# A hybrid decoder block: four projections stream 512 weight columns per matmul, tile by tile

## The chip, the cores and the metric

The kernel runs on one core of a Trainium2 chip. The metric is the device time of one execution in microseconds (us), less being better; the figure of a kernel is the median of its runs. A core has five engines with queues of their own: TensorE (PE), VectorE (DVE), ScalarE (ACT), GpSimd (POOL) and SyncE (SP), which here issues nearly all the loads. They meet only at semaphores.

## What is computed

One layer for 256 tokens of width 1024. `[u | q | k | v | g_pool | g_attn] = RMSNorm(x) @ W_in`; q, k and v feed a stick-breaking attention of 8 heads, u a pooling mixer; the two results are gated, summed into `merged`, and multiplied by `W_out`. Then a top-4-of-32 mixture of experts follows, whose weights (12 MB per expert) are nearly all the bytes that the kernel reads.

```python
h = rmsnorm(x, norm1_g)
u, q, k, v, g_pool, g_attn = split(h @ w_in)
merged = sigmoid(g_pool) * pool_out + sigmoid(g_attn) * attn_out
x = x + merged @ w_out
x = x + moe_ffn(rmsnorm(x, norm2_g), ...)
```

## The kernel before

**Blocks of weights.** The dense part works on twelve blocks of weights in the order q, k, v, u, gp0, gp1, pool_up, ga0, ga1, attn_up, out0, out1 (numbers 0 to 11). A block is 1024 x 512, 2 MB, and lies in SBUF as two halves of 256 columns, each half as eight rows k (one for each 128 of the contraction) of 256 columns. SP loads half h of block b with one DMA of 1 MB into buffer `raw[b % 5]`. ACT copies it to `w_hi[b % 2]` in the type fp32r (`split`, L496), and DVE subtracts that from `raw` in place, which gives `w_lo` (`split`, L626 by its helper). Each half that DVE has done counts in `s_lo` (name `rests_done`). The activations `act_in` have a first part and a rest as well, so a product takes three matmuls (`mm3`: first part by first part, first part by rest, rest by first part).

**The projections.** `project` handles q, k, v, out0 and out1, where the activations are the weights of the array (128 x 128) and the weight block streams past. T = 2 tiles of 128 tokens and KD = 8 rows k give, for each half of the columns, 16 products or 48 matmuls of 256 columns; a block takes 96. The first half goes row by row (k outside, tile inside) and needs only half 0 of the block; the second goes tile by tile and waits for half 1. After the first half PE counts `s_first`, after each tile of the second `done` (`s_proj` or `s_wo`). For out0 the first half takes rows k as `merged` appears (`merged_there`, semaphore `s_mrg`, name `merged_ready`). In v the transposes of the normed k (`transposed(kn)`, L1042) stand between the halves.

**The units.** Between v and out0 PE works through 20 units (attention, u, gates, pool_up, attn_up) in an order written out by hand. In the last four, attn_up, DVE forms `merged` from each unit and splits it in two (L626 onto `act_in`, which counts `s_mrg`); in DVE's program these come ahead of the second half of block 10, which is out0 (`split(10, TWO)`), and that ahead of both halves of block 11 (`split(11)`).

**Buffers and loads.** `used(b, h)` names the semaphore value at which half h of block b is free; SP waits for it before it loads block b + 5, and, since the expert ring `gate_ring` lies over the same memory, before each of 16 gate loads of 1 MB of the first two experts: the second expert's first four wait for out0's halves, its last four for out1's. Then come four loads into `down_ring` (1 MB each), and from there the expert loop: SP reloads a slot each time PE has used it (`s_gu`, `s_du`).

**After out1.** DVE adds x to the four output quarters (`x1`), PE transposes it, and a short chain of small steps on all engines finds the experts (router, ranks, places), after which PE enters the loop over pairs of experts.

Of the kernel before, what the change touches and what calls it, by code (L numbers as in the profile page):

```python
# [5 lines left out]
P = 128  # L6
# [18 lines left out]
def hybrid_block_kernel(nc, x, norm1_g, w_in, q_norm_g, k_norm_g, w_pool_grp, pool_scale, w_pool_up,  # L25
# [4 lines left out]
    T = S // P  # L30
    KD = D // P
# [22 lines left out]
    with ExitStack() as ctx:  # L54
# [49 lines left out]
        NRAW, NHI, BW = 5, 2, KD * BLK  # L104
# [7 lines left out]
        w_lo = [buffer(f"w_lo{j}", j, F32R) for j in range(NRAW)]  # L112
        w_hi = [buffer(f"w_hi{j}", HI_AT + j, F32R) for j in range(NHI)]
# [22 lines left out]
        kn = carve(area_m, 2176, T, BLK)  # L136
# [49 lines left out]
        bank = [ctx.enter_context(nc.psum_tensor(f"bank{i}", [P, 512], F32)) for i in range(8)]  # L186
# [6 lines left out]
        BLOCKS = ["q", "k", "v", "u", "gp0", "gp1", "pool_up", "ga0", "ga1", "attn_up", "out0", "out1"]  # L193
# [11 lines left out]
        s_proj, s_first = sem("projected"), sem("first_half_projected")  # L205
# [6 lines left out]
        s_wo, s_x1, s_hn = sem("out_proj_done"), sem("x1_ready"), sem("hn_ready")  # L212
# [33 lines left out]

        def used(b, h):

            if BLOCKS[b] in ("q", "k", "v"):
                return (s_first, b + 1) if h == 0 else (s_proj, 2 * b + 2)  # L250
            if BLOCKS[b] in ("out0", "out1"):
                return (s_first, b - 6) if h == 0 else (s_wo, 2 * b - 18)
            unit = UNITS.index((BLOCKS[b], 0))
            if BLOCKS[b] in ("pool_up", "attn_up"):
                return s_unit, unit + 2 * h + 2
            return s_unit, unit + h + 1
# [21 lines left out]
        PROJ = (6, 2, 4)  # L278
        TR = (0, 6)
# [691 lines left out]
        def _(pe):  # L971
# [8 lines left out]
            for k in range(KD):  # L980
                for t in range(T):
                    last = nc.tensor.transpose(bank[k // 2][:, (k % 2) * S + t * P:(k % 2) * S + (t + 1) * P],
                                               xn[:, t, k * P:(k + 1) * P], ident[:])
            last.then_inc(s_xT, 1)

            def mm3(o, stat, mov, start):

                mm(o, stat[0], mov[0], start)
                mm(o, stat[0], mov[1], False)
                return mm(o, stat[1], mov[0], False)  # L990
# [6 lines left out]
            def acts(k, cols_at=0, n=S):  # L997
                return act_in[:, 0, k, cols_at:cols_at + n], act_in[:, 1, k, cols_at:cols_at + n]

            def wait_split(b, h):  # L1000

                pe.wait_ge(s_lo, pieces(b)[h][2])

            HB = BLK // 2

            def project(b, banks, ready, done, between=None):

                for t, k in [(t, k) for k in range(KD) for t in range(T)]:
                    if t == 0:
                        ready(k)  # L1010
                        if b == 0 and k % 4 == 0:
                            pe.wait_ge(s_lo, k // 4 + 1)
                        if b and k == 0:
                            wait_split(b, 0)
                    last = mm3(banks[t][:, 0:HB], acts(k, t * P, P), weights(b, 0, k * HB, HB), k == 0)
                last.then_inc(s_first, 1)
                if between:
                    between()
                for t in range(T):
                    for k in range(KD):  # L1020
                        if t == 0 and b == 0 and k % 4 == 0:
                            pe.wait_ge(s_lo, k // 4 + 3)
                        if t == 0 and b and k == 0:
                            wait_split(b, 1)
                        last = mm3(banks[t][:, HB:BLK], acts(k, t * P, P), weights(b, 1, k * HB, HB), False)
                    last.then_inc(done, 1)

            def no_wait(k):
                pass

            def hT_there(k):
                pe.wait_ge(s_hT, k + 1)
# [5 lines left out]
            def transposed(src, b, count):  # L1038
                pe.wait_ge(s_qkn, count)
                for a in range(PAIRS):  # L1040
                    for t in range(T):
                        last = nc.tensor.transpose(  # L1042
                            bank[b + a // 2][:, (a % 2) * S + t * P:(a % 2) * S + (t + 1) * P],
                            src[:, t, a * P:(a + 1) * P], ident[:])
                last.then_inc(s_tr, 1)

            project(0, bank[PROJ[0]:PROJ[0] + T], hT_there, s_proj)
            project(1, bank[PROJ[1]:PROJ[1] + T], no_wait, s_proj)
            transposed(qn, TR[0], T)
            project(2, bank[PROJ[2]:PROJ[2] + T], no_wait, s_proj, lambda: transposed(kn, TR[1], 2 * T))  # L1050

            pe.wait_ge(s_const, 7)
            pe.wait_ge(s_qk, 6)
# [1 line left out]
            for n, (name, j) in enumerate(UNITS):  # L1055
                t = STEP.get(n, -1)
                if 0 <= t - 2 < PAIRS:

                    pe.wait_ge(s_prob, 2 * (t - 2) + 2)
                    for key in range(T):  # L1060
                        for half in range(2):
                            h = 2 * (t - 2) + half
                            o = bank[head_bank(h)][half * HD:(half + 1) * HD, :]
                            last = mm(o[:, key * P:S], vn[:, key, h * HD:(h + 1) * HD],
                                      attn_prob[:, half, key * S:(key + 1) * S - key * P], key == 0)
# [21 lines left out]
                for half in range(2):  # L1087
# [7 lines left out]
                    b = BLOCKS.index(name)  # L1095
# [14 lines left out]
                        last = mm3(dst, weights(b, j, k * HB + half * P, P), acts(k), half == 0 and k == 0)  # L1110
                last.then_inc(s_unit, 1)

            for n in range(2):
                project(BLOCKS.index(f"out{n}"), [acc[n], acc[2 + n]], no_wait if n else merged_there, s_wo)

            for t in range(T):
                pe.wait_ge(s_x1, t + 1)
# [166 lines left out]
```

## Time and profile before

| | |
|---|---|
| median of 3 runs | 1133.45 us (1132.58 to 1134.44) |
| the profiled execution: span | 1132.6 us |
| its own time | 1132.58 us, the lowest of the three |
| PE busy | 1026.0 us, 91% |
| DVE busy | 278.0 us, 25% |
| ACT busy | 187.8 us, 17% |
| DMA | 431.01 MB, mean 381 GB/s |

The profile is of one execution. Its page has the busy time of the engines, the span cut into 40 slices with the granted TensorE clock and the DMA rate, the chain of work that ended last, the costliest groups of instructions and the DMA issues. The trace behind it has each instruction with start, duration and what ended the idle time before it, and it can be asked for stretches of time. PE matmuls overlap: the distance between two starts is shorter than the duration of one.

### The profile page before, as it was taken

The page shows a single profiled execution, that of the slowest core. Times are in us where ns is not written, and L with a number is a line of the kernel's source. Part 1 is how long each engine was busy: PE and PEld are TensorE (multiplying, and loading weights), DVE is VectorE, ACT ScalarE, POOL GpSimd, SP SyncE. Part 2 cuts the span into 40 slices and gives each one's busy share as a digit, 9 for nine tenths or more (in the row PEclk, how much of TensorE's full clock was granted, in tenths as well). Part 3 has the DMA queues.
Part 4 walks back from the last instruction along what each step waited for, and adds up shares of the span by engine and source line. Part 5 has one row for each costly group of instructions (what it writes and reads, how often), then busy time and mean ns, then how long its engine had stood idle before and what let it go on. Part 6 is the DMA issues. An engine that isn't in the chain of part 4 may idle for free.

```text
span 1132.6 us, 14659 instructions
## 1 busy us (share of the span) xinstructions
PE 1026.0 (91%) x5749; PEld 479.0 (42%) x5749; DVE 278.0 (25%) x516; ACT 187.8 (17%) x252; POOL 22.2 (2%) x36
## 2 busy tenths in 40 slices
PE   6999997999999888999989898888888988888897
PEld 6989995333333232333333333232323232233332
DVE  5655886211111111111111111111111010111112
ACT  5477433011101010101010101000010100010101
POOL 3200002000000000000000000000000000000000
PEclk9999998999999999999999999999999999999999
DMA  9933578899999999999999999999999999999996
GB/s 315 322 121 126 186 291 340 327 418 419 417 417 417 418 418 413 417 419 418 418 419 418 417 417 418 417 418 418 417 417 418 417 419 418 418 419 419 418 417 247
DMA packets 97330, 431.01 MB, mean 381 GB/s; under 512 B 7884, under 2 KB 28896, under 8 KB 64512
## 3 DMA queue, kind: packets, MB, share of 16 engines
q1 hardware_dynamic: 97304, 430.76, 94.7%
q8 instruction: 13, 0.21, 0.1%
q14 instruction: 5, 0.04, 0.0%
q10 hardware_dynamic: 8, 0.00, 0.0%
HBM read 429.68 MB, written 1.05 MB: 380 GB/s over the span
## 4 chain that ended last, share of the span: by engine, by line
PE 39%; DMA 27%; SPq 24%; DVE 6%; issue 3%; ACT 0%; POOL 0%; ACTq 0%; DVEq 0%; POOLq 0%
PE bank L973 38%; DMA gate_ring<-in_w_gate_up_dram 22%; SPq L329 11%; SPq L386 9%; DMA down_ring<-in_w_down_dram 4%; SPq L370 3%; DVE area_x L954 1%; PE bank L1238 1%; DVE area_m L626 1%; DVE area_x L938 1%; DVE area_x L626 1%; DVE area_x L939 1%; SPq L378 0%; DMA area_x<-in_x_dram 0%; DVE down_ring L626 0%
## 5 line engine op out<-in xcount | busy, mean ns | idle before, releaser
L973 PE MATMUL bank<-gate_ring,area_m 128*64 128x512 f32 x2048 | 466.3, 597 | 49.1 <-DMA gate_ring<-in_w_gate_up_dram 49.1
L973 PEld LDWEIGHTS bank<-gate_ring,area_m 128*64 128x64 f32 x2048 | 140.0, 136 | 357.1 <-issue 206.9
L973 PE MATMUL bank<-down_ring,area_x 128*64 128x512 f32 x1024 | 230.5, 600 | 24.3 <-DVE area_x L954 13.7
L938 DVE TENSOR_SCALAR area_x<-bank 128x512 f32<-128x512 f32 x32 | 22.1, 692 | 743.2 <-PE bank L973 743.2
L973 PEld LDWEIGHTS bank<-down_ring,area_x 128*64 128x64 f32 x1024 | 72.3, 137 | 163.8 <-issue 142.4
L973 PE MATMUL bank<-area_m 128*128 128x128 bf16 (+4 forms) x1024 | 121.9, 277 | 1.3 <-ACT area_m L609 1.3
L601 ACT ACTIVATE area_x<-area_x 128x512 f32<-128x512 f32 x32 | 20.2, 630 | 489.9 <-DVE area_x L938 489.9
L973 PEld LDWEIGHTS bank<-area_m 128*128 128x128 bf16 (+3 forms) x1024 | 77.5, 114 | 55.9 <-issue 52.1
L609 ACT ACTIVATE area_m<-bank 64x512 f32<-64x512 f32 x64 | 37.8, 591 | 311.4 <-PE bank L973 311.0
L973 PE MATMUL bank<-w_hi,act_in 128*128 128x256 f32 x320 | 59.9, 288 | 1.5 <-DVE act_in L662 1.5
L973 PE MATMUL bank<-act_in,w_hi 128*128 128x256 f32 x320 | 58.4, 284 | 0.0
L626 DVE TENSOR_TENSOR w_lo<-raw,w_hi 128x2048 fp32r<-128x2048 f32 (+1 forms) x26 | 54.7, 2127 | 6.4 <-ACT w_hi L496 6.1
L973 PEld LDWEIGHTS bank<-w_hi,act_in 128*128 128x128 f32 x320 | 51.3, 196 | 1.9 <-DVE act_in L662 1.9
L973 PEld LDWEIGHTS bank<-act_in,w_hi 128*128 128x128 f32 x320 | 49.8, 192 | 0.2 <-DVE area_m L757 0.2
L496 ACT ACTIVATE w_hi<-raw 128x2048 fp32r<-128x2048 f32 (+1 forms) x26 | 45.2, 1778 | 7.6 <-DMA raw<-in_w_in_dram 4.1
L973 PE MATMUL bank<-w_lo,act_in 128*128 128x256 f32 x160 | 45.9, 287 | 0.0
L973 PE MATMUL bank<-act_in,w_lo 128*128 128x256 f32 x160 | 45.3, 283 | 0.0
L973 PEld LDWEIGHTS bank<-w_lo,act_in 128*128 128x128 f32 x160 | 31.4, 196 | 0.0
L973 PEld LDWEIGHTS bank<-act_in,w_lo 128*128 128x128 f32 x160 | 30.7, 192 | 0.0
L954 DVE COPY area_x<-bank 128x512 f32<-128x512 f32 x32 | 22.1, 692 | 27.9 <-PE bank L1238 27.9
L1238 PE MATMUL bank<-ident,area_x 128*128 128x128 f32 x128 | 19.6, 276 | 9.9 <-DVE area_x L626 9.9
L626 DVE TENSOR_TENSOR area_m<-bank,cols 128x512 f32<-128x512 f32 x34 | 23.2, 684 | 2.4 <-PE bank L973 2.4
(171 smaller groups left out, 477.0 us busy)
## 6 DMA issues: line engine op xcount, KB each, us to landing
gate_ring<-in_w_gate_up_dram SPq DMA_DIRECT2D x256, 1024.0 KB, 20.1
down_ring<-in_w_down_dram SPq DMA_DIRECT2D x128, 1024.0 KB, 23.4
raw<-in_w_in_dram SPq DMA_DIRECT2D x16, 1024.0 KB, 10.2
raw<-in_w_out_dram SPq DMA_DIRECT2D x4, 1024.0 KB, 5.1
raw<-in_w_pool_up_dram SPq DMA_DIRECT2D x2, 1024.0 KB, 11.6
raw<-in_w_attn_up_dram SPq DMA_DIRECT2D x2, 1024.0 KB, 4.9
area_x<-in_x_dram SPq DMA_DIRECT2D x2, 512.0 KB, 3.8
out_dram<-gate_ring SPq DMA_DIRECT2D x4, 256.0 KB, 2.1
```

Source lines behind the costliest of these rows:

```text
L329: sp.dma_start(gate_ring[:, s, :], w_gate_up[0, bass.ds(e, 1), c * P:(c + 1) * P, :].rearrange("a p n -> (a p) n")) \
L370: sp.dma_start(down_ring[:, c], down_src(2 * i + half - 1, c)).then_inc(s_dl[c], 16)
L386: sp.dma_start(down_ring[:, c], down_src(e, c)).then_inc(s_dl[c], 16)
L496: nc.scalar.activation(w_hi[b % NHI][:, lo:lo + n], raw[b % NRAW][:, lo:lo + n], ACT.Copy) \
L601: nc.scalar.activation(sig, glu, ACT.Sigmoid, scale=ALPHA).then_inc(s_sig, 1)
L609: last = nc.scalar.activation(y_pair[half * SLOTS:(half + 1) * SLOTS, c * FH:(c + 1) * FH], y_b[c * SLOTS:(c + 1) * SLOTS, :], ACT.Copy)
L626: return nc.vector.tensor_tensor(o, a, b, op)
L938: nc.vector.tensor_scalar(glu, glu_b[:], LIMIT, None, ALU.min).then_inc(s_glu, 1)
L939: nc.vector.tensor_scalar(lin, lin_b[:], LIMIT, -LIMIT, ALU.min, ALU.max).then_inc(s_sr, 1)
L954: nc.vector.tensor_copy(actT, t_b[:].rearrange("p (a n) -> p a n", n=P)).then_inc(s_actT, 1)
L973: return nc.tensor.matmul(o, lhsT, rhs, start=start, stop=True, skip_group_check=True)
L1238: last = nc.tensor.transpose(t_b[:, c * P:(c + 1) * P], lin[:, c * P:(c + 1) * P], ident[:])
```

## The change

`project` is written anew. q keeps the old form under the name `project_halves`. k, v and out1 use the new `project`: it waits once for half 1 of the block (both halves are then there, since `s_lo` counts in order), and then does tile 0 whole and tile 1 whole, each as 24 matmuls of 512 columns; the moving operand takes 256 columns of row k from each half (`weights_row`). out0 uses `project_by_row`: the same matmuls, with k outside and the tile inside, and the waits for `merged` as before. A block takes 48 matmuls in place of 96. In v the transposes of kn stand after tile 0. `s_first` is counted only by q; `used` gives both halves of k, v, out0 and out1 free at the block's end.

```diff
         def used(b, h):
+            if b == 0 and h == 0:
+                return s_first, 1
             if BLOCKS[b] in ("q", "k", "v"):
-                return (s_first, b + 1) if h == 0 else (s_proj, 2 * b + 2)
+                return s_proj, 2 * b + 2
             if BLOCKS[b] in ("out0", "out1"):
-                return (s_first, b - 6) if h == 0 else (s_wo, 2 * b - 18)
+                return s_wo, 2 * b - 18
...
+            def weights_row(b, k):
+
+                return [w[:].rearrange("p (h x) -> p h x", h=2)[:, :, k * HB:(k + 1) * HB]
+                        for w in (w_hi[b % NHI], w_lo[b % NRAW])]
+
+            def project(b, banks, done, between=None):
+
+                wait_split(b, 1)
+                for t in range(T):
+                    for k in range(KD):
+                        last = mm3(banks[t][:].rearrange("p (h n) -> p h n", h=2), acts(k, t * P, P),
+                                   weights_row(b, k), k == 0)
+                    last.then_inc(done, 1)
+                    if between and t == 0:
+                        between()
+
+            def project_by_row(b, banks, ready, done):
+
+                wait_split(b, 1)
+                for k in range(KD):
+                    ready(k)
+                    for t in range(T):
+                        last = mm3(banks[t][:].rearrange("p (h n) -> p h n", h=2), acts(k, t * P, P),
+                                   weights_row(b, k), k == 0)
+                        if k == KD - 1:
+                            last.then_inc(done, 1)
...
-            project(0, bank[PROJ[0]:PROJ[0] + T], hT_there, s_proj)
-            project(1, bank[PROJ[1]:PROJ[1] + T], no_wait, s_proj)
+            project_halves(0, bank[PROJ[0]:PROJ[0] + T], hT_there, s_proj)
+            project(1, bank[PROJ[1]:PROJ[1] + T], s_proj)
             transposed(qn, TR[0], T)
-            project(2, bank[PROJ[2]:PROJ[2] + T], no_wait, s_proj, lambda: transposed(kn, TR[1], 2 * T))
+            project(2, bank[PROJ[2]:PROJ[2] + T], s_proj, lambda: transposed(kn, TR[1], 2 * T))
...
-            for n in range(2):
-                project(BLOCKS.index(f"out{n}"), [acc[n], acc[2 + n]], no_wait if n else merged_there, s_wo)
+            project_by_row(BLOCKS.index("out0"), [acc[0], acc[2]], merged_there, s_wo)
+            project(BLOCKS.index("out1"), [acc[1], acc[3]], s_wo)
```

On PE, at the start of out0, these stand in a row before; `bank0` and `bank2` are the two tiles' results, and `rests_done` is here half 0 of the block.

```order
L973 MATMUL bank7<-mix_in_61,w_hi1_60 128x256 x2
L973 MATMUL bank7<-mix_in_61,w_lo4_58 128x256
L973 MATMUL bank0<-w_hi0_59,act_in_62 128x256 [waits rests_done,merged_ready]
L973 MATMUL bank0<-w_lo0_54,act_in_62 128x256
L973 MATMUL bank0<-w_hi0_59,act_in_62 128x256
L973 MATMUL bank2<-w_hi0_59,act_in_62 128x256
L973 MATMUL bank2<-w_lo0_54,act_in_62 128x256
```

The same place on PE of the changed kernel.

```order
L975 MATMUL bank7<-mix_in_61,w_lo4_58 128x256
L975 MATMUL bank0<-w_hi0_59,act_in_62 128x512 [waits merged_ready,rests_done]
L975 MATMUL bank0<-w_lo0_54,act_in_62 128x512
L975 MATMUL bank0<-w_hi0_59,act_in_62 128x512
L975 MATMUL bank2<-w_hi0_59,act_in_62 128x512
L975 MATMUL bank2<-w_lo0_54,act_in_62 128x512
```

The order of the products is the same, each has 512 columns, and `rests_done` is now the count of half 1, whose instruction on DVE is the second half of block 10.

On DVE the instructions around it stand as before, in both kernels; these are the changed kernel's rows from the last part of `merged` on.

```order
L628 TENSOR_TENSOR area_m<-bank7,area_m 128x512 [waits attn_gate_ready,unit_done]
L628 TENSOR_TENSOR area_m<-area_m 128x512 [waits unit_evacuated]
L628 TENSOR_TENSOR act_in_62<-area_m,act_in_62 128x512 [waits merged_sum,merged_hi]
L628 TENSOR_TENSOR w_lo0_54<-raw0_49,w_hi0_59 128x2048 [waits first_parts_done]
L628 TENSOR_TENSOR w_lo1_55<-raw1_50,w_hi1_60 128x2048 [waits first_parts_done] x2
```

Nothing moved on DVE: PE's first matmul of out0 now waits for the `w_lo0` row here, which stands behind the last `act_in` row, and before it waited for a half done earlier.

## Rows read from the trace of the kernel before

**Rows 1.** Page, chain that ended last: shares of the span by engine and line

```profile
PE 39%; DMA 27%; SPq 24%; DVE 6%; issue 3%; ACT 0%; POOL 0%; ACTq 0%; DVEq 0%; POOLq 0%
```

**Rows 2.** Windows: stretch, its us, busy us of each engine, granted clock, DMA share, GB/s

```profile
158.50:194.00 35.50, 29.33 (x204) 23.56 (x203) 26.70 (x53) 10.28 (x15) 7.75 (x9) 0.87 0.99 401
194.00:203.00 9.00, 8.23 (x82) 6.10 (x82) 3.34 (x18) 1.87 (x2) 0.00 (x0) 0.93 0.03 14
206.00:1110.00 904.00, 821.81 (x4198) 299.40 (x4194) 138.25 (x280) 81.54 (x124) 0.00 (x0) 1.00 1.02 418
```

**Rows 3.** Timeline of SP's DMA issues, 145 to 203 us: start, us, line, tiles, count

```profile
147.76 18.09 SPq L325 DMA_DIRECT2D gate_ring<-in_w_gate_up_dram  x8
...
177.41 11.16 SPq L334 DMA_DIRECT2D down_ring<-in_w_down_dram  x4
202.73 0.36 SPq L329 DMA_DIRECT2D gate_ring<-in_w_gate_up_dram  x1
```

**Rows 4.** Timeline, PE and its weight loads (PEld), inside k

```profile
29.26 0.40 PE L973 MATMUL bank<-w_hi,act_in 128*128 128x256 f32 x2
29.38 0.19 PEld L973 LDWEIGHTS bank<-w_lo,act_in 128*128 128x128 f32 x1
29.50 0.28 PE L973 MATMUL bank<-w_lo,act_in 128*128 128x256 f32 x1
```

**Rows 5.** Timeline of PE at the head of the loop: 512 columns

```profile
200.65 13.91 PE L973 MATMUL bank<-gate_ring,area_m 128*64 128x512 f32 x64
214.49 3.70 PE L973 MATMUL bank<-area_m 128*128 128x512 f32 x8
```

**Rows 6.** Timeline of PE from the end of k to the attention

```profile
39.10 1.03 PE L1042 MATMUL bank<-ident,area_m 128*128 128x128 f32 x8
39.89 0.36 PE L973 MATMUL bank<-w_hi,act_in 128*128 128x256 f32 x1
...
45.72 1.04 PE L1042 MATMUL bank<-ident,area_m 128*128 128x128 f32 x8
...
53.27 0.89 PE L973 MATMUL bank<-area_m,down_ring 128*128 128x256 f32 x4 [0.78 <-ACT area_m L520]
```

**Rows 7.** Timeline of DVE, 19 to 52 us

```profile
19.86 4.70 DVE L626 TENSOR_TENSOR w_lo<-raw,w_hi 128x2048 fp32r<-128x2048 f32 x2 [0.27 <-ACT w_hi L496]
...
33.67 4.48 DVE L626 TENSOR_TENSOR w_lo<-raw,w_hi 128x2048 fp32r<-128x2048 f32 x2
...
40.00 0.69 DVE L674 TENSOR_REDUCE tiny<-down_ring 128x8 f32<-128x512 f32 x1 [1.25 <-ACT down_ring L516]
...
43.97 1.29 DVE L626 TENSOR_TENSOR area_m<-bank,tiny 128x512 f32<-128x512 f32 x2 [3.07 <-POOL tiny L416]
...
48.69 3.09 DVE L697 TENSOR_SCALAR down_ring<-bank,cols 64x512 f32<-64x512 f32 x4
```

**Rows 8.** Timeline of PE where out0 begins

```profile
153.33 0.28 PE L973 MATMUL bank<-w_hi,act_in 128*128 128x256 f32 x1
```

**Rows 9.** Timeline of DVE, 155 to 163 us

```profile
155.65 0.69 DVE L626 TENSOR_TENSOR act_in<-area_m,act_in 128x512 fp32r<-128x512 f32 x1 [0.70 <-ACT act_in L566]
156.26 6.69 DVE L626 TENSOR_TENSOR w_lo<-raw,w_hi 128x2048 fp32r<-128x2048 f32 x3
```

**Rows 10.** Timeline of PE, start of q

```profile
14.52 0.58 PE L973 MATMUL bank<-w_hi,act_in 128*128 128x256 f32 x1 [1.50 <-DVE act_in L662]
...
17.04 0.63 PE L973 MATMUL bank<-w_hi,act_in 128*128 128x256 f32 x2
...
17.68 0.47 PE L973 MATMUL bank<-w_hi,act_in 128*128 128x256 f32 x2
```

**Rows 11.** Timeline of PE between out1 and the loop

```profile
176.37 2.04 PE L1119 MATMUL bank<-ident,down_ring 128*128 128x128 f32 x16
...
189.50 0.21 PE L973 MATMUL bank<-area_m,below_bf 128*128 128x32 bf16 x1 [4.11 <-DVE area_m L845]
```

**Rows 12.** Windows, columns as in group 2

```profile
189.50:195.30 5.80, 5.80 (x27) 3.49 (x28) 3.55 (x19) 0.00 (x0) 0.00 (x0) 0.50 0.83 331
195.30:200.00 4.70, 4.13 (x54) 3.62 (x51) 3.34 (x18) 0.74 (x2) 0.00 (x0) 1.00 0.00 2
```

More of the change, by code:

```diff
@@ L1004, in _, with project_halves @@
             HB = BLK // 2
-            def project(b, banks, ready, done, between=None):
+            def project_halves(b, banks, ready, done):
                 for t, k in [(t, k) for k in range(KD) for t in range(T)]:
@@ L1010, in project @@
                         ready(k)
-                        if b == 0 and k % 4 == 0:
+                        if k % 4 == 0:
                             pe.wait_ge(s_lo, k // 4 + 1)
-                        if b and k == 0:
-                            wait_split(b, 0)
                     last = mm3(banks[t][:, 0:HB], acts(k, t * P, P), weights(b, 0, k * HB, HB), k == 0)
                 last.then_inc(s_first, 1)
-                if between:
-                    between()
                 for t in range(T):
                     for k in range(KD):
-                        if t == 0 and b == 0 and k % 4 == 0:
+                        if t == 0 and k % 4 == 0:
                             pe.wait_ge(s_lo, k // 4 + 3)
-                        if t == 0 and b and k == 0:
-                            wait_split(b, 1)
                         last = mm3(banks[t][:, HB:BLK], acts(k, t * P, P), weights(b, 1, k * HB, HB), False)
                     last.then_inc(done, 1)
-            def no_wait(k):
-                pass
+            def weights_row(b, k):
[19 more added lines that the diff above has]
+                            last.then_inc(done, 1)
             def hT_there(k):
```

## The prediction

> **What bounds the kernel now.** I read three views in this order. The chain that ended last gives PE 39% and the DMAs with their issues most of the rest [rows 1], which says only that the limit changes on the way. The windows say where: from 206 to 1110 us the DMA engines are full, at 418 GB/s, and PE, at 2.4 GHz throughout, has time to spare [rows 2]. So the loop over experts is a stream of bytes of fixed length, and nothing that PE does in it shortens it. But just before it, from 194 to 203 us, the DMA moves 14 GB/s [rows 2]: SP has issued its four loads of `down_ring` by 188.6 us and issues nothing until 202.73, when PE has used up the first gate slot [rows 3]. The rings are full and wait for PE. The end is therefore the start of the loop on PE (200 us) plus a fixed stream, and each us won or lost on PE's path up to 200 us counts whole. In the dense part PE runs from 53.27 us to 176.37 with no idle time before any instruction; its only waits between the start of q and out1's end are 1.5 us at 14.52 and 0.78 at 53.27 [rows 6, 10, 11]. The DVE and ACT steps of the units follow PE's and move with it. So the sum is made on PE.
>
> **The base.** The profiled execution took 1132.6 us, the lowest of the three; the median is 0.9 above it. The sum below is a difference to the profiled execution and is then put on the median.
>
> **Half as many matmuls, twice as long.** Each of four blocks (k, v, out0, out1) goes from 96 matmuls of 256 columns to 48 of 512. Before, starts are 0.12 us apart: two from 29.26 to 29.50 [rows 4], so a block takes 96 x 0.12 = 11.52 us. What one of 512 takes in fp32r no row shows. At the start of q three matmuls take 0.64 us, 0.2133 each [rows 10], which is 256 columns at 1.2 GHz to the last digit; at 2.4 GHz the stream alone would be 0.1067, and 0.12 is 13 ns above it. If these 13 ns are a charge per matmul, 512 columns cost 0.2133 + 0.0133 = 0.2267. If they are the pace of something beside the stream, they vanish under 512 columns. The weight loads suggest the second: they start one for each matmul and take 0.19 each, overlapping [rows 4], and at half the clock, where each has more time, the excess is gone. The nearest row of 512 columns is the gate group of the loop: 64 matmuls in 214.49 - 200.65 = 13.84 us, 0.216 each [rows 5], though with weights of 64 columns. Bounds are 0.2133 (stream alone) and 0.24 (no gain). I take 0.216: 48 x 0.216 = 10.37 us for a block, 1.15 less, and 4.6 for four. With 0.2267 it is 0.64 for a block, 2.55 in all.
>
> On this the Trainium skill (TensorE: Matmul & The Clock Gate, Back-to-back issue gap) gives N / 2.4 GHz + 2.5 ns for the warm gap, thus 216 ns at 512 columns, in accord with the gate group; its 109 ns at 256 is not what this kernel's 0.12 shows, and by the page's own two figures the four blocks would win only 192 x 2.5 ns = 0.5 us. Since the row contradicts the 109, the sum does not use it.
>
> **k.** It now waits for both halves of its weights. PE enters k at 39.10 - 11.52 = 27.6 us, and DVE has split both by 19.86 + 4.70 = 24.56 [rows 7]; q's end is untouched, so nothing is lost. Gain 1.15.
>
> **v.** It starts after the transposes (39.10 to 39.89 [rows 6]), now at 38.7. It needs the second half of its weights; DVE finishes that at 33.67 + 4.48 = 38.15 [rows 7], hidden by 0.6 us, and no step of k stands ahead of it. The transposes of kn stand after tile 0. Before, kn was ready at 43.97 + 1.29 = 45.26 and PE came at 45.72 [rows 6, 7]. The chain of kn hangs on k's end (the reduction at 40.00 waits for ACT's square of k [rows 7]) and moves up 1.15, to 44.1; PE moves up 1.15 for k and 0.58 for half of v, and 24 x 0.216 = 5.18 after 38.7 is 43.9. PE waits about 0.2. The last step before the attention, ACT's copy of v, hangs on v's end [rows 6], and DVE's kz, which ended at 51.78 [rows 7], moves up to 50.6, half a us before PE asks. Gain of k and v: 2.3 - 0.2 = 2.1.
>
> **Loads.** pool_up's first half and ga0's first half are issued 5 us later or less, in a stretch where they are needed tens of us later: nothing. The second expert's gate loads are issued at out0's and out1's ends, four each, in place of two at each half. The backlog behind out1 grows from 2 + 4 MB to 4 + 4, that is 8.4 MB at 417 GB/s, 20.1 us; before, out1's end at 176.4 lay 26.3 us ahead of the first reload at 202.73 [rows 3, 11]. The rings are still full some 6 us before the loop asks: nothing, if that distance is kept.
>
> **out0, the added wait.** Here the cost lies. out0 starts at 153.33 [rows 8] on rows k of `merged` already there, while DVE still has the last of it to do. Now it waits for the second half of its weights. DVE does this after the last part of `merged`: the last `act_in` step ends at 156.34, and the three splits that follow take 6.69 from 156.26, 2.23 each [rows 9]; the first ends at about 158.55. PE starts at 158.6: 158.6 - 153.33 = 5.25 us idle. The whole frame has moved up by the 2.1, since DVE's steps there follow PE's units, and the gap stays. Nothing covers it: PE has no other work queued, the router and the loop stand behind it. Both other waits are void: `merged` is complete, and out1's weights come at 162.95, four us before out0 ends.
>
> **The clock after it.** After its wait of 4.11 us at 189.50 [rows 11] PE got a clock of 0.50, 1.2 GHz, for 5.8 us [rows 12]; at the start of q it ran dense at 0.2133 per 256 columns from 14.52 to 17.7, 3.2 us [rows 10]. So 5.25 us idle is likely to bring the low level, and half of the low stretch is lost: 1.6 us by the start of q, 2.9 by the later row. The start of q is the nearer, the same dense stream; I take 1.6 and keep 0 and 2.9 as ends. The Trainium skill (TensorE: Matmul & The Clock Gate, HAM oscillation) speaks against the change here as well: a pause before a matmul group makes the group run cold. The trace agrees at 189.50.
>
> **Sum.** k and v -2.1, the wait +5.25, the clock +1.6, out0 and out1 -2.3: +2.45 us. Tile by tile in out1 changes nothing, since x1 and the router wait for its last tile. Profiled execution 1135.0, median 1133.45 + 2.45 = 1135.9.
>
> **Rivals.**
> (A) The clock holds at out0. For it: a fall depends on more than the length of a pause. Against: both pauses above were shorter and came with the low level. Then 5.25 - 4.4 = +0.85: 1134.3, not slower. 12%.
> (B) The clock is low at out0 and then not low at 189.50, since PE's work and pauses have moved against whatever the clock goes by. Place: the 5.8 us at 0.50 before the loop [rows 12], on PE's path; if they ran at 2.4 GHz, 2.9 come back: 2.45 - 2.9 = -0.45, 1133.0, not slower. It decides from the point where over 0.2 us of that stretch is at 2.4 GHz, since the forecast stands just there. Against: the pause of 4.11 is DVE's and stays. 20%, mostly by halves (1134.5). With (A) as well it would be 1131.4, faster; 5%.
> (C) The 13 ns are a charge per matmul, or reading two pieces 256 columns apart costs as much: 0.2267 gives 2.55 for all four, no wait at kn: 5.25 + 1.6 - 2.55 = +4.3, 1137.8; at 0.24 (the change does not do what it says) +6.85, 1140.3. For it: all fp32r rows have the 13 ns. Against: the gate group. 15%.
> (D) A long low stretch, 2.9 in place of 1.6: +3.75, 1137.2. 10%.
> The forecast has the other 38%, from 1135 to 1136.8.
>
> **How the numbers follow.** A measurement of this kernel can tell about 0.2%, 2.3 us, from no change: slower is above 1135.7, faster below 1131.2. The forecast sits on that line; I give two thirds of it to slower. Slower: 0.25 + 0.15 + 0.10, and a little of (B)'s rest, 0.52. Faster: 0.06. Same: 0.42. The range leaves out the extreme of (C) and the fullest of (B): 1133.3 to 1138.2.
>
> **What would show it.** In the new profile: matmuls of 512 columns with starts 0.216 apart (or 0.227, or 0.24); k and v together 2.1 shorter, the attention starting at 51.2; PE idle 5.2 us ahead of out0, released by DVE's L628 (its split, two lines further down now); the starts 0.427 apart for about 3 us after it; out1's end 2.4 later than 176.4; DMA idle again before the loop. The prediction is wrong if DVE's second half comes before PE asks, if the loop's first loads find the rings not yet full, or if the stream of two pieces has its own price.

## The result

The changed kernel is slower than before, and by more than was forecast.

| kernel | median us (lowest to highest) | before on the same chip | ratio, 95% interval |
|---|---|---|---|
| changed | 1140.11 (1139.17 to 1140.37) | 1133.95 | 1.0048 [1.0034, 1.0062] |

The forecast was 1135.9 with a range of 1133.3 to 1138.2; the direction was right, the time is 1.9 us above the range. The profiled execution of the changed kernel has a span of 1138.0 us, 5.4 more than before's 1132.6.

One thing about the base has to be put right first. In every run whose span is known here the time is the span plus 2.0 us (the changed kernel: 1138.0 and 1140.03, 1137.2 and 1139.17). So the profiled execution of before took about 1134.6 us, above its median, and was none of the three runs listed; the lowest of them, 1132.58, happened to equal the span. On other chips the kernel before had medians of 1134.5 to 1134.9 (27 and 29 runs each). By the ratio the change costs 5.4 us (3.9 to 7.0), by the two medians 6.2; the difference of the two profiled spans, also 5.4, is what the traces have to account for.

The timeline of PE in the changed kernel, at the places of [rows 4, 6, 8, 11]; in it the old line 973 is 975.

```profile
33.97 0.39 PE L975 MATMUL bank<-w_lo,act_in 128*128 128x512 f32 x1
34.20 0.62 PE L975 MATMUL bank<-w_hi,act_in 128*128 128x512 f32 x2
34.65 0.39 PE L975 MATMUL bank<-w_lo,act_in 128*128 128x512 f32 x1
...
52.80 0.89 PE L975 MATMUL bank<-area_m,down_ring 128*128 128x256 f32 x4 [0.78 <-ACT area_m L522]
...
152.73 0.28 PE L975 MATMUL bank<-mix_in,w_lo 128*128 128x256 f32 x1
158.10 0.80 PE L975 MATMUL bank<-w_hi,act_in 128*128 128x512 f32 x1 [5.10 <-DVE w_lo L628]
158.70 0.63 PE L975 MATMUL bank<-w_lo,act_in 128*128 128x512 f32 x1
...
182.20 2.04 PE L1139 MATMUL bank<-ident,down_ring 128*128 128x128 f32 x16
...
187.65 1.88 PE L975 MATMUL bank<-area_x,ident 128*128 128x512 f32 x4
195.33 0.21 PE L975 MATMUL bank<-area_m,below_bf 128*128 128x32 bf16 x1 [5.80 <-DVE area_m L847]
...
195.68 3.78 PE L975 MATMUL bank<-area_x,ident 128*128 128x512 f32 x4
...
205.63 0.63 PE L975 MATMUL bank<-bias_up,sel_item 96*64 96x512 bf16 x4 [0.77 <-issue]
```

Three matmuls of 512 columns take 34.65 - 33.97 = 0.68 us, 0.2267 each. The idle time ahead of out0, released by DVE's split, is there. From it to the loop's start everything lies 5.44 us later than before (205.63 against 200.19). DVE's timeline at the same place has the row that PE waits for, the first of the three splits.

```profile
155.16 0.69 DVE L628 TENSOR_TENSOR act_in<-area_m,act_in 128x512 fp32r<-128x512 f32 x1 [0.69 <-ACT act_in L568]
155.76 6.69 DVE L628 TENSOR_TENSOR w_lo<-raw,w_hi 128x2048 fp32r<-128x2048 f32 x3
```

Windows of the changed kernel over out0 and out1 (columns as in [rows 2]): PE has 1.2 GHz for the first 4.6 us after the wait and 2.4 GHz from there.

```profile
158.00:162.70 4.70, 4.60 (x11) 3.63 (x12) 4.70 (x4) 0.73 (x1) 0.00 (x0) 0.50 0.87 366
162.70:182.20 19.50, 19.50 (x87) 16.05 (x86) 7.18 (x8) 1.15 (x2) 0.00 (x0) 1.00 0.50 198
```

The stages of the two profiled executions, beside the forecast:

| term | forecast us | measured us | from |
|---|---|---|---|
| up to the start of k | 0 | +0.69 | k starts at 27.58 before and 28.27 after; 0.66 of it lies ahead of q, which starts at 14.52 and 15.18 |
| k and v | -2.1 | -1.16 | attention at 53.27 and 52.80, less the 0.69 |
| wait ahead of out0 | +5.25 | +5.25 | 152.85 (when the last unit's matmul makes room) to 158.10 |
| out0 and out1, columns | -2.3 | -1.28 | 96 x (0.24 - 0.2267) |
| out0, clock | +1.6 | +2.34 | 182.20 - 158.10 = 24.10, less 96 x 0.2267 |
| out1's end to the loop | 0 | -0.39 | 23.82 and 23.43 |
| sum | +2.45 | +5.45 | |

The start of q differs because the first weights landed later in that execution: ACT, which waits for them, began their copy at 11.19 us in place of 10.20. That is not the change's doing: PE's wait at that place was anything from 1.5 to 2.3 us over the profiles of all kernels here, whatever was changed in them.

**What single executions add.** q is the same code in all fourteen profiles, and yet from its first matmul to k's it takes 13.05 to 13.38 us in nine of them, before and changed among these, and 11.61 or 11.62 in the other five (out0_only, keep_busy, before_warm, early_warm5, one_piece). The nine have 3 to 4 us of matmuls at 1.2 GHz in it, the five have none. So two profiles can differ by 1.4 to 1.8 us ahead of the change; where such a pair is compared below, the text says so. Before and the changed kernel differ by only 0.04 there.

### The profile page after: what moved, and what is told of

Same layout as the page of the kernel before. It is cut to its first block, busy times and chain, and to the rows that moved or that the text cites. A ratio compares the mean times of both kernels' runs of the same rounds, so it can differ in the third digit from the quotient of the medians.

```text
span 1138.0 us, 14275 instructions
## 1 busy us (share of the span) xinstructions
PE 1024.0 (90%) x5557; PEld 469.8 (41%) x5557; DVE 277.7 (24%) x516; ACT 187.8 (17%) x252; POOL 22.7 (2%) x36
## 4 chain that ended last, share of the span: by engine, by line
PE 40%; SPq 26%; DMA 24%; DVE 5%; issue 3%; ACT 0%; ACTq 0%; DVEq 0%
PE bank L975 39%; DMA gate_ring<-in_w_gate_up_dram 22%; SPq L331 12%; SPq L388 9%; SPq L372 4%; DMA down_ring<-in_w_down_dram 2%; DVE area_x L956 1%; PE bank L1258 1%; DVE area_m L628 1%; DMA raw<-in_w_in_dram 1%; DVE area_x L940 1%; DVE area_x L628 1%; DVE area_x L941 1%; DVE w_lo L628 0%; SPq L380 0%
## 5 line engine op out<-in xcount | busy, mean ns | idle before, releaser
L975 PE MATMUL bank<-w_hi,act_in 128*128 128x512 f32 (+1 forms) x192 | 55.1, 372 | 7.4 <-DVE w_lo L628 5.1
L975 PEld LDWEIGHTS bank<-w_hi,act_in 128*128 128x128 f32 x192 | 36.3, 202 | 13.2 <-DVE w_lo L628 5.3
L975 PE MATMUL bank<-w_lo,act_in 128*128 128x512 f32 (+1 forms) x96 | 35.5, 370 | 0.0
L975 PE MATMUL bank<-mix_in,w_hi 128*128 128x256 f32 x128 | 23.1, 283 | 0.0
```

Of the source, the lines that this page charges most:

```text
L975: return nc.tensor.matmul(o, lhsT, rhs, start=start, stop=True, skip_group_check=True)
```

## Experiments

All of these are compared with the kernel before on the same chip.

| kernel | median us | before | ratio, 95% interval |
|---|---|---|---|
| kv_only | 1133.53 | 1134.49 | 0.9994 [0.9984, 1.0004] |
| out0_only | 1139.88 | 1134.49 | 1.0060 [1.0046, 1.0074] |
| late_free | 1134.78 | 1134.49 | 1.0005 [0.9996, 1.0014] |
| split_early | 1132.98 | 1134.49 | 0.9990 [0.9981, 0.9999] |
| keep_busy | 1138.00 | 1134.82 | 1.0029 [1.0018, 1.0039] |
| early_warm | 1133.14 | 1134.82 | 0.9986 [0.9973, 0.9999] |
| before_warm | 1135.93 | 1134.82 | 1.0009 [0.9998, 1.0020] |
| early_warm5 | 1130.33 | 1134.91 | 0.9967 [0.9955, 0.9978] |
| before_warm5 | 1132.83 | 1134.91 | 0.9983 [0.9972, 0.9994] |
| early_only | 1135.28 | 1134.91 | 1.0003 [0.9992, 1.0015] |
| one_piece | 1140.28 (one run) | | |
| quarters_v | 1153.50 (one run) | | |

### Which part costs: out0_only, kv_only, late_free

out0_only gives only out0 the new form. In it and in kv_only the other blocks call `halves`, which is the old `project` under another name.

```diff
-            project(1, bank[PROJ[1]:PROJ[1] + T], s_proj)
+            halves(1, bank[PROJ[1]:PROJ[1] + T], no_wait, s_proj)
...
-            project(BLOCKS.index("out1"), [acc[1], acc[3]], s_wo)
+            halves(BLOCKS.index("out1"), [acc[1], acc[3]], no_wait, s_wo)
```

> Only out0 in the new form, k, v and out1 as before. Theory 1: wait 5.2 us, clock 1.6 to 2.9, less 0.64 for out0's 48 matmuls: 6.2 to 7.5 us slower than before, 1140 to 1141.5, idle time ahead of out0 released by DVE's split. Theory 2 (the loss is spread over the four blocks or comes from the loads): 2 us slower or less.

By the ratio it is 6.8 us slower than before (5.2 to 8.4), by the medians 5.4: the whole loss, with the same wait of PE in its list of waits:

```profile
PE bank L981 <- DVE w_lo L634: 5.1, 1, 5.1
```

Theory 1's 6.2 to 7.5 is borne out by the ratio; the median of 1139.88 lies just under the 1140 that it named. The loss is in this block and not spread over four.

kv_only gives only k and v the new form.

> k and v as in the changed kernel, out0 and out1 as before. Theory 1 (each matmul saved is worth 13 ns, all of the loss is out0's wait and the clock after it): 96 matmuls fewer, 1.3 us faster than before, about 1132.6; starts of 512 columns 0.227 apart. Theory 2 (the later free buffers of k and v delay loads that PE then waits for, or k's wait for both halves costs): 0 to 2 us slower than before, with idle time on PE at k, v or the first units.

late_free is the kernel before with only the buffers given free later.

```diff
-                return (s_first, b + 1) if h == 0 else (s_proj, 2 * b + 2)
+                return (s_first, 1) if b == 0 and h == 0 else (s_proj, 2 * b + 2)
...
-                return (s_first, b - 6) if h == 0 else (s_wo, 2 * b - 18)
+                return s_wo, 2 * b - 18
```

> The kernel before, with only the buffers of k, v, out0 and out1 given free at the block's end, as in the changed kernel. Theory 1 (loads are hidden: the rings are full before the loop starts): no change, within 0.5 us of before. Theory 2 (the second expert's gate loads, 5.8 us later each pair, push the stream back): up to 5 us slower.

late_free shows no difference: the later loads cost nothing that can be measured. kv_only has a median 1.0 us under before's, in keeping with 1.3, but its interval includes no change. Its profile has the gain where it was expected: k takes 10.92 us in place of 11.52, and from there to the attention it is 13.66 in place of 14.18, 1.1 us together. It also shows why it is hard to see. q started 0.47 us later in that execution and took 0.20 longer, so out1 ends at 175.91, only 0.46 before the 176.37 of [rows 11]. The loop starts at 198.8, 1.4 before before's 200.19; yet the first reload is issued at 202.61, where [rows 3] have 202.73. Timeline of PE and of SP, and a window (columns as in [rows 2]), in kv_only:

```profile
199.22 10.03 PE L979 MATMUL bank<-gate_ring,area_m 128*64 128x512 f32 x38
```

```profile
202.61 12.72 SPq L335 DMA_DIRECT2D gate_ring<-in_w_gate_up_dram  x8
```

```profile
199.00:203.00 4.00, 4.00 (x14) 1.29 (x12) 0.00 (x0) 0.69 (x1) 0.00 (x0) 0.58 0.01 4
```

The first gate matmuls of the loop ran mostly at 1.2 GHz, so the slots came free as late as before. In the kernel before all of the low stretch had lain ahead of the loop [rows 12], up to 195.3 us; here it ended at 192.8, and a second one came on the gate matmuls. A theory came out of this: the low clock that PE's pause in the router brings falls now here, now there, and takes back part of what is won ahead of it. The totals leave it little: from out1's end to the first reload it is 26.70 us here and 26.36 before, so the other place of the low clock costs 0.3 us. That the low clock itself costs 2 us and more in either kernel is another matter, and is tested further down.

### The cure of the wait: split_early

DVE splits out0's second half at unit 16, two units earlier than the end.

```diff
-                 14: (9, BOTH), 15: (10, ONE)}
+                 14: (9, BOTH), 15: (10, ONE), 16: (10, TWO)}
...
-            split(10, TWO)
             split(11)
```

> The changed kernel, with DVE's split of out0's second half moved up to unit 16, two units before the last attn_up unit is done. Theory 1: no wait ahead of out0 and no fall of the clock, merged's last part comes 2.2 us later at 158.5 but PE asks for it 8 us after out0's start: four blocks win 0.64 each, 2.6 us faster than before, about 1131.3. Theory 2 (the new form itself is slow, or loads push the stream back): slower than before by 2 us or more even so.

The wait is gone, out0 follows the last unit at once. PE's timeline:

```profile
152.69 0.28 PE L974 MATMUL bank<-mix_in,w_lo 128*128 128x256 f32 x1
152.81 0.40 PE L974 MATMUL bank<-w_hi,act_in 128*128 128x512 f32 x1
...
198.28 11.31 PE L974 MATMUL bank<-gate_ring,area_m 128*64 128x512 f32 x44
```

The median is 1.5 us under before's, by the ratio 1.1 (0.1 to 2.2), not 2.6. PE ends out1 at 174.60, 1.8 earlier than before, and starts the loop 2.4 earlier, but SP's first reload comes only 1.5 earlier, and the window has the low clock on the gate matmuls again:

```profile
201.26 2.85 SPq L331 DMA_DIRECT2D gate_ring<-in_w_gate_up_dram  x2
```

```profile
199.00:203.00 4.00, 4.00 (x14) 1.19 (x12) 0.00 (x0) 0.00 (x0) 0.00 (x0) 0.57 0.25 33
```

The four blocks do win what they should in this profile: k and v 1.15 us and out0 and out1 1.25 (21.79 in place of 23.04), 2.4 of the 2.6. Against that stand 0.4 at q's start, 0.2 in the units, which take 100.14 us in place of 99.94 in all four kernels with the moved split, and 0.3 from out1's end to the first reload. From that reload to the end of the span it is 930.9 us in place of 929.9; what the last 1.0 comes from is not shown.

early_only makes the same move in the kernel before.

> The kernel before with only DVE's split of out0's second half moved up to unit 16. Theory 1: PE never waits for it there, no change, within 0.5 us, so that what split_early wins is the 512 columns' own. Theory 2 (the move itself frees something): faster than before by 1 us or more.

No difference in the times: the moved split wins nothing by itself.

### The clock after the wait: keep_busy

The changed kernel with matmuls into a free bank ahead of out0, which end as the wait does.

```diff
+            b10 = BLOCKS.index("out0")
+            wait_split(b10, 0)
+            merged_there(0)
+            for _ in range(22):
+                mm(bank[1][:, 0:HB], acts(0, 0, P)[0], weights(b10, 0, 0, HB)[0], True)
+                mm(bank[1][:, 0:HB], acts(0, 0, P)[0], weights(b10, 0, 0, HB)[0], True)
             project_by_row(BLOCKS.index("out0"), [acc[0], acc[2]], merged_there, s_wo)
```

> The changed kernel, with 44 matmuls of 256 columns into a bank that is not in use put ahead of out0 (5.3 us of work at 2.4 GHz), so that PE works through the wait. The wait stays, the low clock after it should go. Theory 1 (the low stretch of the clock cost 2.3 us in out0): out1's end about 2.3 us earlier than in the changed kernel, 1137 to 1138.5. Theory 2 (only the wait counts, the clock's cost is made up later by the pauses of the router): the same time as the changed kernel, about 1140.

It is 3.2 us slower than before by the medians, 3.3 by the ratio (2.0 to 4.4), where the changed kernel is 5.4 slower by the ratio. Timeline of PE and a window: the added matmuls run from 150.97 together with the first of out0, the rest of out0 and out1 has 2.4 GHz all through, and out1 ends at 178.12, 21.6 us after 156.56, where out0's second matmul starts.

```profile
150.97 5.76 PE L975 MATMUL bank<-w_hi,act_in 128*128 128x256 f32 x45
156.56 0.40 PE L975 MATMUL bank<-w_lo,act_in 128*128 128x512 f32 x1
...
178.12 2.04 PE L1145 MATMUL bank<-ident,down_ring 128*128 128x128 f32 x16
```

```profile
158.30:178.00 19.70, 19.70 (x89) 16.32 (x88) 9.71 (x10) 1.15 (x2) 0.00 (x0) 1.00 0.59 237
```

In the changed kernel the same piece took 182.20 - 158.70 = 23.5 us. So 1.9 us of the 2.34 go with the idle time; the rest is the first matmul of out0, 158.70 - 158.10 = 0.60 in the changed kernel against 0.23. The low clock after the wait is the wait's doing. How much it costs varies with the same wait ahead of it: 1.5 us in out0_only (23.91 for out0 and out1, less 48 x 0.2267 and 96 x 0.12), 1.9 in quarters_v, 2.1 in one_piece, 2.3 in the changed kernel.

### The clock in the router's pause: early_warm, before_warm, early_warm5, before_warm5

After out1 PE adds x to the output banks by f32 matmuls, the residual matmuls, first for one tile of tokens; then it pauses until the ranks can be counted, and then come the residual matmuls of the other tile. These kernels put more matmuls into the pause, nine in the first two and five in the others.

```diff
             residual(0)
+            for _ in range(5):
+                mm(bank[7][:], ident[:], x_sb[:, 0, 0:FH], True)

             pe.wait_ge(s_sel, 1)
```

> split_early, with nine f32 matmuls of 512 columns (4 us) into a bank that is not in use put into PE's pause of 5.8 us before the ranks are counted. Theory 1 (the gain of the four blocks was taken back by a low stretch of the clock in the second residual matmuls and in the loop's first gate matmuls, which the pause brings about): no low clock from there to the loop, first reload 2 us or more earlier than in split_early, 1130 to 1131.5. Theory 2 (the end does not follow the loop's start, the DMA stream has slack): same time as split_early, 1133.

> The kernel before with the same nine matmuls in the pause. Theory 1: 2 to 3 us faster than before, 1131 to 1132.5, since the second residual matmuls and the first gather run at 2.4 GHz. Theory 2: no change. With split_early and early_warm it tells what the four blocks win when the clock is the same in both: 2.6 us by 13 ns for each matmul saved.

Nine were too many. PE's timeline in early_warm:

```profile
180.06 9.61 PE L974 MATMUL bank<-area_x,ident 128*128 128x512 f32 x22
189.51 0.18 PE L974 MATMUL bank<-area_m,below_bf 128*128 128x32 bf16 x1
```

The two residual matmuls and the nine added ones stand as 22 rows of 0.43 us: an f32 matmul is recorded as two. They filled the pause and 1.8 us more. The clock is high throughout this stretch, and from out1's end to the first reload it is 25.69 us in place of split_early's 26.66, the 1.8 included. before_warm came out 1.1 us slower by the median, with an interval that includes no change, and its runs spread from 1132.41 to 1137.70; early_warm won 1.7, not the 3 or more expected.

> split_early with five f32 matmuls of 512 columns in PE's pause before the ranks are counted. The nine of early_warm turned out as 18 records of 0.43 us, 7.7 us of work in a pause of 5.8, so they pushed PE back by 1.8 us; five are 4.3 us. Theory 1 (the low clock at the end of the pause costs 2 us or more): the second residual matmuls start at 187.7 and take 1.9 us, the loop starts at 196, first reload about 198.5, 2.5 us or more faster than split_early, 1129.5 to 1130.5. Theory 2: as split_early.

> The kernel before with the same five matmuls in the pause. Theory 1: 2 to 3 us faster than before; against early_warm5 it tells what the 512 columns win when both have the high clock to the loop's start: 2.6 us. Theory 2 (the clock does not reach the end): no change.

early_warm5 is the fastest kernel here, 4.6 us faster than before by the medians and 3.7 (2.5 to 5.1) by the ratio. Its PE timeline and first reload, in an execution among its fastest (1128.21, the median is 1130.33):

```profile
177.87 6.17 PE L974 MATMUL bank<-area_x,ident 128*128 128x512 f32 x14
185.56 0.19 PE L974 MATMUL bank<-area_m,below_bf 128*128 128x32 bf16 x1 [1.52 <-DVE area_m L846]
...
185.87 1.98 PE L974 MATMUL bank<-area_x,ident 128*128 128x512 f32 x4
...
194.43 13.91 PE L974 MATMUL bank<-gate_ring,area_m 128*64 128x512 f32 x64
```

```profile
196.52 12.33 SPq L331 DMA_DIRECT2D gate_ring<-in_w_gate_up_dram  x8
```

The second residual matmuls take 1.98 where the changed kernel's took 3.78, and the reload comes 6.2 us ahead of [rows 3]. Not all of this is the kernel's: 0.34 is q's earlier start and 1.45 is q's clock, which was high from its first matmul on in this execution; the rows below stand 0.35 apart for three matmuls, where [rows 10] have 0.64. The four blocks win 2.4 and lose 0.2 in the units, and from out1's end to the reload it is 24.11 us in place of 26.36, 2.25 less by the clock.

```profile
14.88 0.40 PE L974 MATMUL bank<-w_hi,act_in 128*128 128x256 f32 x2
...
15.23 0.40 PE L974 MATMUL bank<-w_hi,act_in 128*128 128x256 f32 x2
```
 before_warm5 wins 2.1 (ratio 1.9, 0.7 to 3.2), and in its profiled execution the low clock was not kept off: its pause shows one low stretch and the loop's head another, and from out1's end to the reload it is 24.96 us, 1.4 less than before.

```profile
182.46 7.87 PE L973 MATMUL bank<-area_x,ident 128*128 128x512 f32 x14
...
198.95 10.46 PE L973 MATMUL bank<-gate_ring,area_m 128*64 128x512 f32 x40
```

```profile
199.00:203.00 4.00, 4.00 (x14) 1.25 (x12) 0.00 (x0) 0.34 (x1) 0.00 (x0) 0.60 0.01 2
```

The medians of the two differ by 2.5 us on one chip, the ratios by 1.8. The 2.6 of 192 matmuls at 13.3 ns lies there, but each ratio is uncertain by 1.3 us to either side, so the times alone do not settle it. The stages of the traces do, with 2.4 in each profile that has all four blocks in the new form and no wait.

### What a matmul of 512 columns costs: one_piece, quarters_v

one_piece streams 512 columns side by side in place of two pieces, and writes the output bank in one piece too. It takes other columns of the block than the kernel needs, and only its times count.

```diff
-                return [w[:].rearrange("p (h x) -> p h x", h=2)[:, :, k * HB:(k + 1) * HB]
+                return [w[:, k * BLK:(k + 1) * BLK]
                         for w in (w_hi[b % NHI], w_lo[b % NRAW])]
```

> The changed kernel, with 512 weight columns that lie side by side in place of two pieces of 256 (so the products of k, v, out0 and out1 use other columns of the block than they should). Theory 1 (a charge of 13 ns for each matmul of this kind): starts 0.227 us apart as in the changed kernel. Theory 2 (the two pieces cost 11 ns): 0.216 apart.

PE's timeline in it, inside k:

```profile
34.08 0.62 PE L975 MATMUL bank<-w_hi,act_in 128*128 128x512 f32 x2
34.54 0.39 PE L975 MATMUL bank<-w_lo,act_in 128*128 128x512 f32 x1
34.76 0.62 PE L975 MATMUL bank<-w_hi,act_in 128*128 128x512 f32 x2
```

34.76 - 34.08 = 0.68 for three, 0.2267 as with two pieces. The pieces cost nothing.

quarters_v gives v matmuls of 128 columns.

```diff
+                        for c in range(4):
+                            lo = (c % 2) * P
+                            last = mm3(banks[t][:, c * P:(c + 1) * P], acts(k, t * P, P),
+                                       weights(b, c // 2, k * HB + lo, P), k == 0 and c == 0)
```

> The changed kernel, with v streamed in matmuls of 128 columns (192 in place of 48), everything else as it is. Theory 1 (a fixed charge of 13 ns on top of the stream for each matmul): starts 0.067 us apart, v takes 12.8 us. Theory 2 (a floor of 0.12 us, the pace of the weight loads, which 256 columns just touch): 0.12 apart, v takes 23 us.

```profile
43.86 0.38 PE L975 MATMUL bank<-w_hi,act_in 128*128 128x128 f32 x2
...
45.87 0.39 PE L975 MATMUL bank<-w_hi,act_in 128*128 128x128 f32 x2
```

Eighteen matmuls lie between the two rows, 2.01 / 18 = 0.112 us each. Neither theory was right as it stood: 128 columns are held to 0.112, more than their stream of 0.053 and 13 ns; 256 take 0.120 and 512 take 0.2267, each its stream and 13.3 ns. So there is a floor at 0.112 and a charge of 13.3 ns above it, and at 256 columns it is already the charge that counts. What sets the floor no run shows.

## Why the prediction was wrong, step by step

**What bounds the kernel** held. The span ends 929.9 us after the first reload before (1132.6 and 202.73) and 929.8 in the changed kernel (1138.0 and 208.17); over all kernels here it is 929.7 to 932.0, while the reload itself moves by 23 us (196.52 in early_warm5, 219.49 in quarters_v). The end follows the first reload, to within 2.3 us. It does not follow PE's loop start as closely: the first gate matmuls lie between the two, and their clock moves the reload by up to 1.5 us (2.54 us from the loop's start to the reload before, 4.07 in keep_busy). "Each us won or lost on PE's path up to 200 us counts whole" was too short a path by those matmuls.

**The wait ahead of out0** was right, with its place, its releaser and its cause. That 5.25 us agrees to the hundredth is luck; DVE's step alone was rounded by 0.05.

**The price of 512 columns** is the step that failed: "I take 0.216". The trace has 0.2267. The row it was taken from, 64 matmuls in 13.84 us, was misread. The code has 32 matmuls there (8 rows, two banks, two halves of columns) and the row says x64: f32 matmuls are recorded twice, each record 0.43 us long when it has the array alone, as in [rows 5], 3.70 us for the x8 of four matmuls. With weights of 64 columns the records start in pairs, 0.012 us apart, and the next pair 0.43 later. So the 0.216 is what two column halves of the array, working side by side, make of 0.43; no matmul of 512 columns had run in 0.216, and the figure that the prediction sets beside the gate group is not borne out by it. A count of the row against the loop of the code would have shown it. The other value, 13 ns as a charge, was in the text as rival (C), with 1137.8 for the time, and was given 15%. The sum was off by 3.0 us, and this term is 192 x (0.2267 - 0.216) = 2.05 of them (k and v won 0.94 less than forecast, though the wait of 0.2 at kn did not occur, and out0 and out1 1.02 less). The Trainium skill (FP8 and Floating Point Precision, TensorE Precision Notes) says that true FP32 takes 4 passes through the array; by an estimate from that, 4 x 512 columns at 2.4 GHz are 0.853 us, and the two records of 0.43 agree.

**The clock after the wait** came as forecast and was sized too low for this execution: 2.34 in place of 1.6, between the two ends named (0 and 2.9). keep_busy shows that it goes with the idle time, and the four profiles with the wait have 1.5 to 2.3. The row that the 1.6 was taken from was the wrong one: at the start of q the clock did not fall in the pause of 1.5 us, it was low before it. The transposes ahead of that pause take 3.68 us for 16, where the same number at 2.4 GHz takes 2.04 [rows 11]:

```profile
9.34 3.68 PE L982 MATMUL bank<-ident,down_ring 128*128 128x128 f32 x16 [2.85 <-DVE down_ring L644]
```

(A window over 14.50 to 17.70 us gives a granted clock of 1.00 in that profile; the low clock there is read from the distance of the starts, 0.2133 us.) In out0_only, with the same pause of 1.5 us, q ran at 2.4 GHz from its first matmul. So that the 1.6 came near was luck in part, and of the two pauses that the prediction holds against rival (A) only the one at 189.50 counts.

**Loads** cost nothing, as forecast (late_free).

**The base** was wrong: the profiled execution was taken for the lowest run, by a coincidence of two numbers. It did no harm to the difference, but that was taken from an execution of 1134.6 and put on a median of 1133.45, 1.15 less. With the 3.0 of the terms this makes up the 4.2 between 1135.9 and 1140.1. The price of 512 columns alone would have given 1137.95, just inside the range; price, clock and base together put the time outside it. Medians on other chips lie 0.5 to 1 us above the 1133.95, and that moves the forecast by as much.

**Rival (B)**, that the low clock ahead of the loop goes away, did not happen in the changed kernel: 3.78 us for the second residual matmuls, as before. But its mechanism is real and works the other way as well: in kv_only and split_early part of the low clock lay on the loop's first gate matmuls. The sum hardly changes by that: from out1's end to the first reload it is 26.70 and 26.66 us in these two, 26.36 before and 25.97 in the changed kernel. With the clock high throughout it is 24.11 (early_warm5).

The rest, 0.69 us ahead of k less 0.39 between out1 and the loop, is put down to the scatter of single executions; the 0.39 goes with a low clock of 5.0 us after the ranks in place of 5.8.

## What to carry to other kernels

A wait for a whole block where half a block was enough costs the time until the other half is made (5.25 us here), and what the low clock after the pause costs on top (1.5 to 2.3); look up what stands ahead of that half in the producing engine's program, and move it. Here that, with TensorE kept busy in its next pause, turns a loss of 5.4 us into a gain of about 4 (ratio 0.9967). Larger matmuls win only the charge for each, here 13.3 ns, which is small beside one such wait. Before a row's duration is used as a price, its count has to be held against the loop that issues it.

## What the runs showed of the hardware

- fp32r matmuls with 128 x 128 weights, back to back at 2.4 GHz: 0.112 us with 128 columns, 0.120 with 256, 0.2267 with 512; at 1.2 GHz 0.2133 with 256. Two pieces of 256 cost as much as one of 512.
- f32 matmuls stand in the profile as two records each, 0.43 us apart with 512 columns; f32 transposes as one (16 in the code, x16 in [rows 11]). Two f32 matmuls with weights of 64 columns on the two halves of the array run at the same time.
- PE idle for 5.1 us: 1.2 GHz in the 4.6 us of work that follow, 2.3 us lost; 3.0 us and 1.5 lost after the same wait in out0_only. Filled with matmuls, out0 and out1 run at 2.4 GHz throughout.
- PE idle for 5.8 us before a light stretch: the low clock falls on that stretch and, in seven of the eight profiles with that pause, once more on the loop's first gate matmuls. Five f32 matmuls in the pause are worth 2 us to the kernel before (ratio 1.9) and about 3 to split_early (-4.6 against -1.5 by the medians on two chips, 2.6 by the ratios and in the traces).
- The start of q has the clock at 1.2 GHz for 3 to 4 us in nine profiles and not at all in five, by the distance of the starts, with 13.05 to 13.38 against 11.6 us for q. The transposes before it ran at 1.2 GHz in all of them, but for the last few in early_warm5 and before_warm.
- Why single executions of one kernel spread by up to 5 us (before_warm 1132.41 to 1137.70) stays open. There is one profile of each kernel; if the low stretches come and go between runs of one kernel as they do between the profiles, they explain 1 to 3 of them.
